# A streaming encoder layer: rotation partners of queries and keys moved 64 partitions apart, query norms taken up in the scores' scale

## The chip, the cores and the metric

One NeuronCore of one Trainium2 chip runs the whole layer in one launch. The metric is the device time of that launch in microseconds (us), the median of several runs. A profiled execution is one more run, with the hardware profiler's records; its span goes from the first to the last instruction.

## The reference, cut to what matters

The kernel computes one layer for 1024 prompt tokens and 32 tokens of a running stream, 1056 in all: two token mixers (windowed attention with sinks, a gated linear recurrence), their merge, and a SwiGLU feed-forward part. Everything is float32. The part that the change touches is what happens to queries and keys between the input projection and the attention scores:

```python
q = partial_rope(rms_norm(q.reshape(B, T, N_HEADS, HEAD_DIM), q_norm), positions)
k = partial_rope(rms_norm(k.reshape(B, T, N_KV_HEADS, HEAD_DIM), k_norm), positions)
# rms_norm: x * rsqrt(mean(x*x) + 1e-6) * gain, over the 64 features of a head
# partial_rope: of the 64 features, the first 16 are rotated, feature d (0..7) with its partner d+8
x1, x2 = xr[..., : ROT_DIM // 2], xr[..., ROT_DIM // 2:]
rot = jnp.concatenate([x1 * cos - x2 * sin, x2 * cos + x1 * sin], axis=-1)
# attention: each chunk of 64 tokens sees its own chunk and the one before
s = jnp.einsum('bnqkgd,bnskd->bnkgqs', q, k).astype(jnp.float32) * ATTN_SCALE
m = jnp.maximum(jnp.max(s, axis=-1, keepdims=True), sink)
p = jnp.exp(s - m)
den = jnp.sum(p, axis=-1, keepdims=True) + jnp.exp(sink - m)
```

There are 16 query heads and 4 key and value heads of 64 features, so four groups of four query heads share one key head.

## The kernel before, in words

Activations lie by features: 128 features on the partitions, 1056 tokens along the free dimension, cut into three blocks of 352 tokens (`BW`). A float32 product is made of three TensorE products of a split form (high times high, high times low, low times high); GpSimd makes the high and low parts of each weight unit (128 x 1024 numbers) in `split` (L494), in two halves of 512, one rounding copy (L501) and one subtraction (L503) each. Two units are held, so a unit can be split once the unit two before it has been used up. The first 52 units (`EARLY`) are split so; a block of 352 tokens of one unit is `dense_block` (L589): 24 products of 128x128 weights with 352 columns.

The stages, in order of time: loads and the first norm; four rounds of the recurrence's front; the values (nine jobs on tokens as rows); six blocks of keys (two units of 128 features, each with two heads, times three token blocks); six blocks of queries for group 0; then, for each of the four groups, four units of merge gates (288 products, `group`, L754) with the attention of the group woven in between them, and after each of the first three groups the six query blocks of the next one. From about 694 us on come the large output and feed-forward products. The order of all work is written out by hand in the program of each engine, with semaphores between them.

Around the change, for one block k of keys or queries:

- ScalarE, `qk_copy` (L1034): the squares of the block into `qsq` (L1040), the block times the norm's gain into `qsb` (L1041); both have two buffers, and the copy of block k waits until the rotation products and the cosine product of block k-2 have been done.
- TensorE, `qk_aux` (L691), after the next dense block: two plain float32 products of 352 columns, with `blkones` (ones on each head's 64 x 64 block: sums of squares, already spread over the head's partitions) into `aux0`, and with `perm` (a signed permutation: each feature's rotation partner) into `aux1`. Each is recorded as two matmuls with a weight load of its own.
- ScalarE, `qk_root` (L1043): the square root of the mean into `qstd`.
- VectorE, `rope` (L1458): partner times sine from `aux1` (L1462), `qsb` times cosine (L1463), their sum (L1466), the reciprocal of `qstd` (L1468), and the product with it, into `kst` for keys (L1476) or into `qt` for queries (L1482).

Keys go through DRAM (`store_k`, L1048) and come back per group into `kg` (`load_group`, L1076), which holds two copies of the group's key head, one on the upper and one on the lower 64 partitions, with zeros elsewhere (set once, L1486 and L1487), so that one product gives the scores of two heads. An attention step (`attention_step` in the programs of TensorE L715, ScalarE L1096 and VectorE L1494) handles one chunk u of 64 tokens: scores, row maxima (L1508), the negated maximum with the sink (L1515), `exp` with the scale 1/8 (L1111), the row sums and their reciprocal, the scaled probabilities (L1519), two steps later their transposes (L750), three steps later the product with the values. Steps begin with the 72nd of the group's 288 products and then come every 11 products. `small1` and `small2` hold constants, among them `blkones`, `perm`, the gains and the sinks.

## Time and profile before

| what | us |
|---|---|
| median of 3 runs | 1694.2 |
| the 3 runs | 1694.5, 1689.61, 1694.2 |
| profiled execution, its own time | 1689.04 |
| its span, first to last instruction | 1687.0 |

The granted TensorE clock over the span is 0.992 of full speed. The page of the profile gives the busy time of each engine; matmuls are pipelined, so that a matmul's recorded duration is longer than the distance from its start to the start of the next one. The distance between starts is what TensorE spends.

### The profile page before, as it was taken

How to read it: one execution, taken by the hardware profiler on the slowest of the kernel's cores; microseconds unless marked ns; L12 is line 12 of the kernel's file. 1: busy time of each engine (PE TensorE's matmuls, PEld its weight loads, DVE VectorE, ACT ScalarE, POOL GpSimd, SP SyncE). 2: the span in 40 equal slices, each digit the busy share in tenths (PEclk: the TensorE clock that was granted, in tenths of full speed). 3: DMA queues.
4: the chain of work that ended last, by engine and by line, in shares of the span. 5: the costliest groups of instructions: out<-in, count | busy, mean ns of one | idle time of the engine just before them, and what ended most of it. 6: DMA issues, size and time to landing. Idle time of an engine off the chain costs nothing. (4 is left out here: it accounts for less than half of the span.)

```text
span 1687.0 us, 29106 instructions
## 1 busy us (share of the span) xinstructions
PE 1630.2 (97%) x11242; PEld 1538.5 (91%) x11242; DVE 1056.0 (63%) x1648; ACT 621.0 (37%) x1310; POOL 958.3 (57%) x685
## 2 busy tenths in 40 slices
PE   7899989999999999999898999999999999999999
PEld 4799989988889898898897989999999999998998
DVE  6687674964747565667889778333333334869685
ACT  5444542243343424424234334333333334333242
POOL 5665652222223121377785717877777777786876
PEclk9999999999999999999999999999999999999999
DMA  5011122233123131254441612222242222373634
GB/s 191 26 63 63 57 68 83 67 90 103 55 85 75 68 102 57 99 217 166 153 154 56 200 52 87 91 77 78 81 167 95 77 77 77 141 265 115 254 141 148
DMA packets 72764, 182.12 MB, mean 108 GB/s; under 512 B 14704, under 2 KB 26416, under 8 KB 72000
## 3 DMA queue, kind: packets, MB, share of 16 engines
q1 hardware_dynamic: 51376, 159.13, 26.8%
q10 hardware_dynamic: 21264, 21.27, 4.4%
q8 instruction: 85, 1.39, 0.3%
q14 instruction: 39, 0.32, 0.1%
HBM read 131.36 MB, written 49.28 MB: 107 GB/s over the span
## 5 line engine op out<-in xcount | busy, mean ns | idle before, releaser
L577 PE MATMUL bank<-xh,wsh 128*128 128x264 f32 x2170 | 623.4, 287 | 21.7 <-POOL wsl L553 8.1
L577 PE MATMUL bank<-xh,wsl 128*128 128x264 f32 x2170 | 619.8, 286 | 0.0
L577 PE MATMUL bank<-xl,wsh 128*128 128x264 f32 x2170 | 619.2, 285 | 0.0
L577 PEld LDWEIGHTS bank<-xh,wsh 128*128 128x128 f32 x2170 | 411.5, 190 | 25.3 <-issue 16.1
L577 PEld LDWEIGHTS bank<-xl,wsh 128*128 128x128 f32 x2170 | 411.5, 190 | 0.2
L577 PEld LDWEIGHTS bank<-xh,wsl 128*128 128x128 f32 x2170 | 411.7, 190 | 0.0
L577 PE MATMUL bank<-acth,wh 128*128 128x352 f32 x960 | 320.6, 334 | 4.6 <-POOL actl L509 3.7
L577 PE MATMUL bank<-acth,wl 128*128 128x352 f32 x960 | 311.7, 325 | 0.0
L577 PE MATMUL bank<-actl,wh 128*128 128x352 f32 x960 | 310.2, 323 | 0.0
L501 POOL TENSOR_SCALAR wh<-wraw 128x512 fp32r<-128x512 f32 x100 | 83.7, 837 | 393.6 <-PE bank L577 373.5
L553 POOL TENSOR_TENSOR wsl<-praw,wsh 128x512 fp32r<-128x512 f32 (+1 forms) x157 | 242.5, 1545 | 81.2 <-ACT wsh L1166 81.1
L553 POOL TENSOR_TENSOR wsl<-wsum,wsh 128x512 fp32r<-128x512 f32 (+1 forms) x120 | 186.2, 1552 | 84.8 <-ACT wsh L1166 84.7
L1166 ACT ACTIVATE wsh<-praw 128x512 fp32r<-128x512 f32 (+1 forms) x157 | 97.0, 621 | 260.7 <-PE bank L577 234.9
L577 PEld LDWEIGHTS bank<-acth,wh 128*128 128x128 f32 x960 | 180.3, 188 | 9.5 <-POOL actl L509 4.5
L577 PEld LDWEIGHTS bank<-actl,wh 128*128 128x128 f32 x960 | 180.9, 188 | 3.2
L577 PEld LDWEIGHTS bank<-acth,wl 128*128 128x128 f32 x960 | 180.3, 188 | 0.4
L503 POOL TENSOR_TENSOR wl<-wraw,wh 128x512 fp32r<-128x512 f32 x100 | 148.3, 1483 | 14.6 <-POOL wh L501 0.2
L1741 DVE TENSOR_TENSOR ev<-bank,ev 128x264 f32<-128x264 f32 x126 | 53.8, 431 | 158.9 <-PE bank L577 158.9
L1166 ACT ACTIVATE wsh<-wsum 128x512 fp32r<-128x512 f32 (+1 forms) x120 | 74.2, 619 | 197.6 <-POOL wsum L549 117.0
L1548 DVE TENSOR_TENSOR xl<-acc,xh 128x2112 fp32r<-128x2112 f32 (+1 forms) x47 | 129.7, 2759 | 23.9 <-ACT xh L1183 23.9
L1645 DVE SCALAR_TENSOR_TENSOR ev<-bank,ev 128x264 f32<-128x264 f32 x90 | 38.7, 430 | 136.0 <-PE bank L577 135.3
L549 POOL TENSOR_TENSOR wsum<-praw,wsum 128x512 f32<-128x512 f32 (+1 forms) x45 | 73.2, 1627 | 79.9 <-PE bank L577 79.9
(173 smaller groups left out, 2393.2 us busy)
## 6 DMA issues: line engine op xcount, KB each, us to landing
praw<-in_weights SPq DMA_DIRECT2D x34, 1024.0 KB, 4.8
wraw<-in_weights SPq DMA_DIRECT2D x52, 512.0 KB, 3.3
h_scratch<-ev SPq DMA_DIRECT2D x44, 264.0 KB, 2.0
acc<-h_scratch SPq DMA_DIRECT2D x4, 2112.0 KB, 12.5
ev<-x_scratch SPq DMA_DIRECT2D x6, 1056.0 KB, 4.9
spare<-x_scratch SPq DMA_DIRECT2D x6, 1056.0 KB, 5.0
praw<-in_weights SPq DMA_DIRECT2D x8, 768.0 KB, 4.6
ta_scratch<-tg ACTq DMA_DIRECT2D x24, 176.0 KB, 1.8
```

Of the source, the lines that this page charges most:

```text
L501: nc.gpsimd.tensor_scalar(wh[:, u, c], wraw[:, u, c], 1.0, 0.0, ALU.mult, ALU.add).then_inc(split_done, 1)
L503: nc.gpsimd.tensor_tensor(wl[:, u, c], wraw[:, u, c], wh[:, u, c].bitcast(f32), ALU.subtract)\
L549: nc.gpsimd.tensor_tensor(dst, a, b, op).then_inc(wsum_done, 1)
L553: nc.gpsimd.tensor_tensor(w_slot(wsl, p, r), w_part(p, r), w_slot(wsh, p, r).bitcast(f32), ALU.subtract)\
L577: return nc.tensor.matmul(*args, **kw)
L1166: f(w_slot(wsh, p, r), w_part(p, r), ACT.Copy).then_inc(whi_done, 1)
L1548: V.tensor_tensor(xl[k][:, 0:n, :], x_part(t, k), xh[k][:, 0:n, :].bitcast(f32), ALU.subtract)\
L1645: stt(u2(par, n), bank[BANKS[2][n]][:, 0:QB], scale, u2(par, n), ALU.mult, ALU.add).then_inc(u2_done, 1)
L1741: V.tensor_tensor(dst, bank[BANKS[r][n]][:, 0:QB], (u4(par, n), None, u2(par, n), u2(par, n))[r - 3], ALU.add).then_inc(done, 1)
```

## The change

The features of two heads, which lay as head 0 on partitions 0 to 63 and head 1 on 64 to 127, are laid out anew: of each run of 16 features the first eight go to the lower 64 partitions and the second eight to the upper 64, so that feature d and its partner d+8 lie exactly 64 partitions apart. Head 0 then has partitions 0 to 31 and 64 to 95, head 1 the rest. GpSimd makes this order as it splits the weight units of keys and queries (ten of the 52; the loop over units is written out from the 14th pair of units on). VectorE reads the partner from the other half of the partitions, so the `perm` product is gone. Keys keep their norm as before, with the ones matrix `heads` in the new pattern, now made on the chip. Queries are no longer divided by their norm: ScalarE squares them into a part of `ot` that is free at the time, 17 small products per group sum them (tokens as rows, two columns), and the inverse root comes into the scores' scale and into the negated maximum. Loads and stores that meet the features' order (rotation tables, gains, cached keys, key outputs) are cut up accordingly.

```diff
-KVG_DMAS = 16 * 7
+KVG_DMAS = 16 * 9
+PAIR_ROWS = ROT // 2
+TURNED = (13, 14, 17, 20, 23)
+    def turned(rows):
+        return rows.rearrange("(a s b) t -> s a b t", s=2, b=PAIR_ROWS)
-        small2 = tensor(early, "small2", [P, C_END - C_BLK])
+        small2 = tensor(early, "small2", [P, C_END - C_VEC])
+        heads = tensor(early, "heads", [P, P])
+        gains = tensor(early, "gains", [P, 2])
+            qroot = tensor(s, "qroot", [P, AU, 2])
+            qinv = tensor(s, "qinv", [P, 2, AU, 2])
+        def qsquares(g):
+            return ot[:, g % 2, :, :].rearrange("p i t -> p (i t)")
+        def by_unit(a, n, i):
+            return a[:, 2 * n * BW:2 * (n + 1) * BW].rearrange("p (b i t) -> p b i t", i=2, t=HT)[:, :, i, :]
 GpSimd
+            def turn(half):
+                return half.rearrange("p (c a s b) -> p s c a b", c=4, s=2, b=PAIR_ROWS)
+            def straight(half):
+                return half.rearrange("p (c s a b) -> p s c a b", c=4, s=2, b=PAIR_ROWS)
+                    if turned:
+                        raw, high, low = turn(raw), straight(high), straight(low)
 TensorE
-            def qk_aux(base, k, b, after):
-                wait(pe, free[b], after)
-                wait(pe, std_done, base + k)
-                mm(aux0[:, 0:BW], blkones, qsq[:, k % 2, :], start=True, stop=True).then_inc(ss_done, 1)
-                wait(pe, rot_used, base + k)
-                mm(aux1[:, 0:BW], perm, qsb[:, k % 2, :], start=True, stop=True).then_inc(rot_done, 1)
+            def k_sums(k, b, after):
+                wait(pe, free[b], after)
+                wait(pe, std_done, k)
+                mm(aux0[:, 0:BW], heads[:, :], qsq[:, k % 2, :], start=True, stop=True).then_inc(ss_done, 1)
+            def q_sums(g, job):
+                wait(pe, free[job.bank], job.after)
+                wait(pe, std_done, 6)
+                wait(pe, qroot_done, 2 * g)
+                wait(pe, ot_done, AU * g)
+                for u in range(AU):
+                    q, _, q0 = unit_shape(u)
+                    i = mm(aux0[0:2 * q, 2 * u:2 * u + 2], qsquares(g)[:, 2 * q0:2 * (q0 + q)], heads[:, 0:HD:HD // 2],
+                           start=True, stop=True)
+                i.then_inc(qss_done, 1)
-                    if done[0] == 9:
-                        qk_aux(*late)
+                    if done[0] == 18:
+                        q_sums(g, late)
 ScalarE
-            act.dma_start(kt_dram[:, SEQ:SEQ + KV_CACHED], kc_in[:, WINDOW - KV_CACHED:WINDOW]).then_inc(kv_stored, 16)
+            for i in range(2):
+                for h in range(2):
+                    rows = slice(i * P + h * HD, i * P + (h + 1) * HD)
+                    for j in range(2):
+                        r0 = i * P + j * HD + h * HD // 2
+                        act.dma_start(kt_dram[r0:r0 + HD // 2, SEQ:SEQ + KV_CACHED].rearrange("(a b) t -> a b t", b=PAIR_ROWS),
+                                      turned(kc_in[rows, WINDOW - KV_CACHED:WINDOW])[j]).then_inc(kv_stored, 16)
-            act.dma_start(cs[:, :, :], cs_in).then_inc(cs_loaded, 16)
+            for j in range(2):
+                act.dma_start(cs[j * HD:(j + 1) * HD, :, :].rearrange("p k t -> p (k t)"),
+                              turned(cs_in.rearrange("p k t -> p (k t)"))[j]).then_inc(cs_loaded, 16)
+                wait(act, cos_done, base + k - 1)
+                f(qsb[:, k % 2, :], ps, ACT.Identity, scale=gain).then_inc(copied, 1)
+                if base == 0:
+                    wait(act, ss_done, k - 1)
+                    f(qsq[:, k % 2, :], ps, ACT.Square).then_inc(free[job.bank], 1)
+                else:
+                    g = base // 6 - 1
+                    wait(act, ot_stored[g % 2], 16 * (g // 2))
+                    f(by_unit(qsquares(g), k % NB, k // NB), ps.rearrange("p (b t) -> p b t", t=HT), ACT.Square)\
+                        .then_inc(free[job.bank], 1)
+            def q_root(g):
+                    wait(act, qss_done, g + 1)
+                    wait(act, qinv_done, 4 * g)
+                    f(qroot[rows, units, :], aux0[rows, 2 * units.start:2 * units.stop].rearrange("p (u h) -> p u h", h=2),
+                      ACT.Sqrt, scale=1.0, bias=HD * EPS).then_inc(qroot_done, 1)
-                        f(pr[0:2 * q, r, h, 0:k], sbank[i % 2][0:2 * q, h * P:h * P + k], ACT.Exp, scale=HD ** -0.5,
+                        f(pr[0:2 * q, r, h, 0:k], sbank[i % 2][0:2 * q, h * P:h * P + k], ACT.Exp,
+                          scale=qinv[0:2 * q, 0, i, h:h + 1],
-                qk_root(6 * g + 6, 5)
+                q_root(g)
 VectorE
-                V.tensor_tensor(rt2[:, :], aux1[:, 0:BW], cs[:, 1, x], ALU.mult).then_inc(rot_used, 1)
+                stt(rt2[0:HD, :], qsb[HD:P, k % 2, :], -1.0, cs[HD:P, 1, x], ALU.mult, ALU.mult).then_inc(sin_done, 1)
+                stt(rt2[HD:P, :], qsb[0:HD, k % 2, :], 1.0, cs[0:HD, 1, x], ALU.mult, ALU.mult).then_inc(sin_done, 1)
             def rope_q(base, k):
-                rope(base, k)
+                halves(base, k)
+                V.tensor_tensor(by_unit(qt, k % NB, k // NB), rt1[:, :].rearrange("p (b t) -> p b t", t=HT),
+                                rt2[:, :].rearrange("p (b t) -> p b t", t=HT), ALU.add).then_inc(rope_done, 1)
+            def q_inverse(g):
+                    V.reciprocal(qinv[rows, 0, units, :], qroot[rows, units, :]).then_inc(qinv_done, 1)
+                    V.tensor_scalar(qinv[rows, 1, units, :], qinv[rows, 0, units, :], -1.0, None, ALU.mult).then_inc(qinv_done, 1)
-            V.memset(kg[HD:P, 0, :], 0.0).then_inc(kz_done, 1)
-            V.memset(kg[0:HD, 1, :], 0.0).then_inc(kz_done, 1)
+            for j in range(4):
+                V.memset(kg[j * HD // 2:(j + 1) * HD // 2, 1 - j % 2, :], 0.0).then_inc(kz_done, 1)
-                    stt(sm[rows, r, 1, :], sm[rows, r, 0, :], -HD ** -0.5, snk[rows, 0, :], ALU.mult, ALU.min)\
+                    for h in range(2):
+                        stt(sm[rows, r, 1, h:h + 1], sm[rows, r, 0, h:h + 1], qinv[rows, 1, i, h:h + 1], snk[rows, 0, h:h + 1],
+                            ALU.mult, ALU.min).then_inc(nm0_done, 1)
 SyncE
+            for j in range(2):
+                sp.dma_start(gains[j * HD:(j + 1) * HD, :], turned(small_in[:, C_GAIN:C_SINK])[j]).then_inc(gains_loaded, 16)
...
```

## Rows read from the trace of the kernel before

**Rows 1.** The page's first part: busy time, share of the span, instructions.

```profile
PE 1630.2 (97%) x11242; PEld 1538.5 (91%) x11242; DVE 1056.0 (63%) x1648; ACT 621.0 (37%) x1310; POOL 958.3 (57%) x685
```

**Rows 2.** Busy time by stretch: its ends and length, engines, granted clock, DMA.

```profile
404.00:438.00 34.00, 34.00 (x193) 31.45 (x193) 22.12 (x24) 10.94 (x21) 12.60 (x12) 1.00 0.44 107
...
694.00:1687.00 993.00, 965.37 (x7236) 937.35 (x7234) 606.56 (x767) 338.52 (x553) 706.45 (x457) 0.99 0.37 130
```

**Rows 3.** Timeline of TensorE around one pair of small products: start, us, engine, line.

```profile
326.78 0.32 PE L577 MATMUL bank<-actl,wh 128*128 128x352 f32 x1
...
330.33 0.32 PE L577 MATMUL bank<-acth,wl 128*128 128x352 f32 x1
330.49 0.75 PE L577 MATMUL bank<-qsq,small 128*128 128x352 f32 x2
...
331.83 0.32 PE L577 MATMUL bank<-actl,wh 128*128 128x352 f32 x1
...
336.86 0.32 PE L577 MATMUL bank<-actl,wh 128*128 128x352 f32 x1
```

**Rows 4.** Timeline of TensorE: pairs in the queries of group 1.

```profile
412.14 0.76 PE L577 MATMUL bank<-qsq,small 128*128 128x352 f32 x2
...
432.27 0.75 PE L577 MATMUL bank<-qsq,small 128*128 128x352 f32 x2
```

**Rows 5.** Weight loads: one tile's (ns min/median/max), then a stretch of the timeline.

```profile
L577 PEld LDWEIGHTS bank<-qsq,small x60: 187/188/190, 284.2 to 627.7; 128*128 128x128 f32 x60
...
378.41 0.19 PEld L577 LDWEIGHTS bank<-acth,wl 128*128 128x128 f32 x1
378.52 0.19 PEld L577 LDWEIGHTS bank<-acth,wh 128*128 128x128 f32 x1
```

**Rows 6.** Timeline of VectorE, and of ScalarE's square, in one block of keys.

```profile
304.33 0.53 DVE L1462 TENSOR_TENSOR rt<-bank,cs 128x352 f32<-128x352 f32 x1
304.77 0.52 DVE L1463 TENSOR_TENSOR rt<-qsb,cs 128x352 f32<-128x352 f32 x1
...
306.17 0.46 ACT L1040 ACTIVATE qsq<-bank 128x352 f32<-128x352 f32 x1 [4.08 <-PE bank L577]
...
308.90 0.53 DVE L1462 TENSOR_TENSOR rt<-bank,cs 128x352 f32<-128x352 f32 x1
```

**Rows 7.** Timeline of VectorE and GpSimd at the start of the keys.

```profile
288.50 0.99 DVE L1487 MEMSET kg<- 64x1120 f32 x1 [0.29 <-issue]
...
290.43 1.37 POOL L503 TENSOR_TENSOR wl<-wraw,wh 128x512 fp32r<-128x512 f32 x1
290.75 1.43 DVE L1466 TENSOR_TENSOR rt<-rt 128x352 f32<-128x352 f32 x1
```

**Rows 8.** Timeline of ScalarE at the start, and one later store.

```profile
0.74 0.65 ACTq L890 DMA_DIRECT2D kt_scratch<-in_cache_k  x1
...
2.73 1.28 ACT L896 ACT_TABLE_LOAD   x1 [2.73 <-issue]
...
6.59 2.44 ACT L923 ACTIVATE wg<-wraw,vt 128x128 f32<-128x128 f32 x8 [2.11 <-DMA wraw<-in_weights]
...
305.59 0.45 ACTq L1058 DMA_DIRECT2D out_ks<-kst  x1
```

**Rows 9.** Timeline of GpSimd: a split half, before the keys and in group 1.

```profile
277.05 1.29 POOL L503 TENSOR_TENSOR wl<-wraw,wh 128x512 fp32r<-128x512 f32 x1
...
446.44 0.62 POOL L501 TENSOR_SCALAR wh<-wraw 128x512 fp32r<-128x512 f32 x1 [9.02 <-PE bank L577]
```

**Rows 10.** Timeline of VectorE and TensorE in a running attention step.

```profile
378.52 0.42 DVE L1519 TENSOR_TENSOR pr<-pr,sm 128x256 f32<-128x256 f32 x1
...
381.18 0.44 PE L750 MATMUL bank<-small,pr 128*128 128x128 f32 x2
```

**Rows 11.** Busy time by stretch (as in Rows 2), around a long stall of TensorE.

```profile
764.00:766.00 2.00, 0.00 (x0) 0.00 (x0) 2.00 (x2) 1.00 (x2) 2.00 (x2) 0.85 0.06 23
...
768.00:770.00 2.00, 2.00 (x11) 2.00 (x11) 0.89 (x1) 0.00 (x0) 2.00 (x2) 0.50 0.91 372
```

More of the change, by code:

```diff
@@ L516, in _ @@
             x_low(2)
-            with pool.Fori(2, EARLY_N // 2) as i:
+            with pool.Fori(2, TURNED[0]) as i:
                 for u in range(2):
                     split(i, u, False)
+            for i in range(TURNED[0], EARLY_N // 2):
+                for u in range(2):
+                    split(i, u, False, i in TURNED)
             def w_sum(p, i):
@@ L587, in products, with dense_block @@
                 return mm(out, lhs[1], rhs[0][cols], start=False, stop=last)
-            def dense_block(slot, n, rh, rl, each=None, ahead=0, before=None):
+            def dense_block(slot, n, rh, rl, each=None):
                 job = plan.take(last=n == NB - 1)
@@ L594, in dense_block @@
                     if n == 0 and k % 4 == 0:
-                        weights(ahead, k // 4)
-                    if before:
-                        before(n, k)
+                        weights(0, k // 4)
                     w = slice(k * P, (k + 1) * P)
@@ L702, in qk @@
                         job = dense_block(i, n, acth, actl)
-                        if attended is not None and i == 0 and n == 1:
-                            wait(pe, pt_done, attended)
-                            wait(pe, ot_done, attended)
                         if late:
-                            qk_aux(*late)
-                        late = (base, NB * i + n, job.bank, job.after)
-                return late
-            late = qk(0)
-            late = qk(6, late)
+                            k_sums(*late)
+                        late = (NB * i + n, job.bank, job.after) if keys else None
+                return late or job
+            def q_sums(g, job):
[8 more added lines that the diff above has]
+                i.then_inc(qss_done, 1)
+            pe.wait_ge(heads_done, 5)
+            late = qk(keys=True)
+            late = qk(late)
             def attention_step(g, i):
@@ L1488, in _ @@
+            V.memset(heads[:, :], 0.0).then_inc(heads_done, 1)
+            dve.wait_ge(heads_done, 1)
+            for j in range(4):
+                rows = slice(j * HD // 2, (j + 1) * HD // 2)
+                V.memset(heads[rows, :].rearrange("p (s h n) -> p h s n", s=2, h=2)[:, j % 2], 1.0).then_inc(heads_done, 1)
+            dve.wait_ge(cs_loaded, 32)
+            for j in range(4):
+                V.memset(kg[j * HD // 2:(j + 1) * HD // 2, 1 - j % 2, :], 0.0).then_inc(kz_done, 1)
             for k in range(6):
```

115 lines of the change are left out of this document (56 added, 59 removed).

## The prediction

> **What bounds the kernel now.** I read the page's busy shares first: TensorE works 97% of the span, no other engine above 63% [rows 1], and the granted clock is 1.00 where the change lies and 0.99 in the long stage behind it [rows 2]. So time is won where TensorE spends less, and lost where it waits. Next the timeline of TensorE in a query phase: 22 dense products start between 326.78 and 330.33, 0.161 us apart, so a block of 24 takes 3.87. Then the pair of small products comes: from 330.33 to 331.83 it is 1.50 us for what would be two steps (0.32), so a pair costs 1.18 us, 0.59 a product, in float32 with two passes each [rows 3]. The queries of group 1 bear it out: pairs 0 and 4 stand 20.13 us apart, 5.03 a block, and 5.03 - 3.87 = 1.16 [rows 4]. Third, VectorE beside it: one key block takes it 4.57 us, from the first row to the last [rows 6]. It is just below TensorE's 5.03, so today it keeps up, and it is the engine to watch when TensorE's blocks get shorter. The stage after 694 us starts from TensorE's end of the groups, and TensorE is busy 965 of its 993 us [rows 2]: I let it move as it is.
>
> **Queries, groups 1 to 3.** Each group had six pairs: 6 x 1.17 = 7.0 us go. What comes is 17 products with a stationary operand of 128 squares' columns and two moving columns, two passes each as for every plain float32 product (x2 in [rows 3]), so 34 weight loads with next to nothing between them. The trace has no such series. From below: nothing under the 0.06 us that would be half of the load distance below, 2.0 us a group. From above: a load takes 0.188 us from start to end [rows 5], 6.4 us a group if none overlaps. Nearest is a place where the queue was empty and two full loads follow each other, 378.41 and 378.52: 0.11 us apart [rows 5]; the second began as soon as the first was in place. I take 0.11 plus 0.01 for the short product, 0.12 x 34 = 4.1 us. So a group gains 7.0 - 4.1 = 2.9 us, three groups 8.7.
> VectorE falls from five operations to four short ones per query block: each 0.44 from the next or 0.53 long [rows 6], and not over 0.2 of semaphores between them, about 2.3 us against 3.87, so no query block waits for it. ScalarE's root moves behind the sums: it comes some 7 us into the group, while the first attention step is at product 72, 11.6 us plus the 4.1 in; the two reciprocals and negations are tiny. Cost nothing; cover 8 us.
>
> **Keys and queries of group 0.** A key block keeps one product: TensorE's pace could be 3.87 + 0.59 = 4.46. VectorE now needs 4.57 + 0.44 for the second half of the sine product = 5.01 [rows 6]. So here VectorE becomes the bound: TensorE's sums of block k wait for ScalarE's copy of k, and that waits for the cosine product of k-2. VectorE starts later too: the second memset of `kg` started at 288.50 and lasted 0.99 [rows 7]; there are now four of them, so with 0.4 for the second table load they end about 288.5 + 0.4 + 3 x 0.99 + 0.3 = 292.2. The sums of the sixth key block then need the cosine product of the fourth: 292.2 + 3 x 5.01 + 1.4 (0.44 + 0.44 + 0.52) = 308.6; ScalarE's two operations of 0.46 [rows 6] 0.9, the sums 0.6: 310.1; GpSimd's contention (below) 0.6: 310.7. Five query blocks more are 19.35: group 0 starts at 330.1. Before it started one product ahead of 336.86, at 336.7 [rows 3]. That is 6.6 us gained, and up to product 72 there is 4.1 now against 1.17: 3.7 net. If TensorE kept its own pace of 4.46 through five key blocks, it would be up to 2.8 us better; if each key block cost VectorE 0.5 more, 1.5 to 2.5 worse.
>
> **Start.** ScalarE issues ten loads at the head of its program in place of three, each of its DMA issues from DRAM to DRAM 0.65 us [rows 8]; a store with several strides is 0.45 [rows 8]. Eight by 0.45 to 0.65 replace one: 3.0 to 4.6 us more ahead of the table load at 2.73. That work used to end 2.11 us before the first weights landed at 6.59 [rows 8], so 0.9 to 2.5 us are late, and ScalarE's scaled weights are what the first matmul waits for. I take 1.6 lost. The smaller constant load may give back 0.3.
>
> **GpSimd's new order.** A half takes 0.62 for the copy and 1.29 for the subtraction [rows 9], in runs of 512; the ten turned units read runs of eight. The trace has no such access on this engine. From below no gain (same count of elements); from above I let it take three times as long, 5.7 us a half. Before the query units GpSimd had been idle 9.02 us [rows 9], so even 3 x as long costs little there. The first key unit is not covered, as TensorE waits for its halves: 1.9 us more for each doubling of a half, but VectorE's bound in the keys (start at 292.2) hides about 2.5 us of that. I take 0 (runs of 32 bytes, same engine work), bound 4.
>
> **Attention steps.** One more tiny operation on VectorE (0.1 us) ahead of `exp`. A chunk's probabilities are ready at 378.52 + 0.42 = 378.94 and transposed at 381.18 [rows 10]: 2.2 us of slack. Nothing.
> What works against this cover: in the keys' rows a sum on VectorE lasted 1.43 in place of 0.53 while GpSimd's subtraction ran from 290.43 to 291.80 [rows 6, 7]. The change replaces an operation with one operand in PSUM by two with both in SBUF, so it meets this more often: at most 0.9 us per meeting, two units split in the keys, 0.6 to 2 us; the 0.6 is in the sum above. The Trainium skill (SBUF — State Buffer, section "SBUF: two separate sides") says that the port pair shared by VectorE and GpSimd is an exclusive lock, taken by a VectorE operation with two SBUF inputs; the trace agrees with the 1.43 us. By that rule alone every one of the eight GpSimd operations in the keys would be added to VectorE, and the keys would end 2 us later still.
>
> **Sum.** 8.7 + 3.7 - 1.6 + 0.3 = 11.1 us less. On the profiled execution, 1689.0 - 11.1 = 1677.9. The median shown is 5.2 us above that execution and the fastest run 0.6 above it, so the runs alone scatter by 0.3%, about what a measurement of this kernel can tell from no change; I put the median after at 1694.2 - 11.1 = 1683.
>
> **Rivals.**
> A. The clock falls. In the 4.1 us of the sums TensorE multiplies next to nothing. After a stall in which it stood still (busy 0.00 from 764 to 766), the granted clock went from 1.00 to 0.50, the lower level of 1.2 GHz, and stayed there while it was fully busy from 768 to 770 [rows 11]. Such a fall costs half of some 3.4 us, 1.7 us. Four groups: 6.8 us, so the gain is 4.3 and the time 1690. For it: the products' columns are too few to count. Against it: weights are loaded all the time, and the dense products stand right before and behind. The Trainium skill (TensorE: Matmul & The Clock Gate, "What's actually happening") says that the throttled state is the default and activity releases it; it agrees with the rows, and doesn't settle whether loading counts.
> B. Loads that don't overlap (ends slower). Each small pass waits for its own load to end and the load for the pass before: 0.188 plus some 0.06 of the product, 0.25 us, 136 of them 34 us in place of 16.3. That takes 17.7 us back: slower by 6.6, 1701. It decides from 11.1 + 16.3 = 27.4 us over 136, 0.20 us a pass. For it: the 0.188 of the load [rows 5]. Against it: the 0.11 there.
> C. The loads are cheaper, 0.06 to 0.08 us a pass: 6 to 8 us better, 1676.
> D. The change does less than it says: VectorE's keys and the start cost 5 us more (three times as long turned splits, 0.65 a DMA issue, port waits): 1688.
>
> **How the numbers follow.** Forecast 0.40, A 0.28, B 0.08, C 0.12, D 0.12. The likeliest is 1683. C sets the low end, 1673; A and D with a median that may itself fall 3 us either way set the high end, 1693. Faster by over 0.3% (below 1689): the forecast and C nearly whole, half of D and 0.4 of A, 0.40 + 0.12 + 0.06 + 0.12 = 0.70. Slower: B and a rest of D and A, 0.10. Same 0.20.
>
> **What would show it.** TensorE's count falls by 54 products and rises by 68. The weight loads with `ot` as source stand 0.11 us apart (C: 0.06; B: 0.2 or more). In the keys VectorE has no idle time from about 292 us on, and TensorE waits for ScalarE's square there, some 3 us in all. Query blocks start 3.87 us apart. The first matmul starts 1 to 2 us later than 9.13. Granted clock 1.00 between 320 and 690 (A: below it in four places right behind the sums). Group 0's attention starts about 345 us. The forecast is wrong if the loads cost over 0.16 us each, or if TensorE waits in the query phases for any engine.

## The result, and the profile after

The changed kernel takes 1699.01 us (median of 6 runs, 1698.15 to 1700.86) against 1692.9 before (6 runs, 1689.61 to 1694.5). The ratio is 1.0046 with a 95% interval of 1.0034 to 1.0057: slower by 0.46%. The forecast was 1683 with a range of 1673 to 1693, so it missed, and on the wrong side. The profiled execution has a span of 1696.7 us against 1687.0, and a mean granted clock of 0.984 against 0.992.

The first part of the page, as in [rows 1]: TensorE is busy 5.6 us less in a span that is 9.7 us longer. It waits more.

```profile
PE 1624.6 (96%) x11270; PEld 1544.6 (91%) x11270; DVE 1031.9 (61%) x1721; ACT 626.4 (37%) x1294; POOL 959.2 (57%) x685
```

Three marks on TensorE's timeline divide the difference: the first score product of group 0, the first product of the stage behind the groups, and the end of the span. Before they stand at 349.69, 694.85 and 1687.0, after at 363.13, 707.02 and 1696.7. So up to the first score 13.4 us are lost, in the four groups 1.3 are won (345.16 to 343.89), and behind them 2.5 come back (992.15 to 989.68). By its sum the prediction had 2.4 us won by the first mark (3.7 - 1.6 + 0.3; its "about 345 us" for the first score would be 4.7 and does not fit that sum), and 8.7 between the first two.

Two things limit this account. The profiled execution of the kernel before is its fastest (1689.04 by its own time, median 1692.9), that of the changed kernel lies at its median, so the marks divide 9.7 us where the medians differ by 6.1. And the code behind the groups is the same in all fourteen kernels of this document, while that stage lasts 989.6 to 993.5 us in their traces: the 2.5 us are within that scatter.

**Start.** Timeline of ScalarE (ACT, its DMA queue ACTq) and TensorE (columns: start, us, engine, line), beside [rows 8]:

```profile
0.74 6.96 ACTq L930 DMA_DIRECT2D kt_scratch<-in_cache_k  x8
7.74 0.63 ACTq L932 DMA_DIRECT2D out_ks<-in_cache_k  x1
...
9.26 1.28 ACT L937 ACT_TABLE_LOAD   x1 [9.26 <-issue]
...
10.92 2.43 ACT L964 ACTIVATE wg<-wraw,vt 128x128 f32<-128x128 f32 x8
...
13.44 0.93 PE L606 MATMUL bank<-acc,wg 128*128 128x352 f32 x1 [13.44 <-ACT wg L964]
```

Eight issues take 0.87 us each. The table load starts 6.5 us later than before, the scaled weights 4.3 later, and the first product at 13.44 in place of 9.13.

**Keys.** Timeline of all engines in the keys of group 0; compare the starts with [rows 6, 7]:

```profile
285.17 1.41 ACTq L1073 DMA_DIRECT2D cs<-in_rope  x2
...
297.50 0.99 DVE L1562 MEMSET kg<- 32x1120 f32 x1 [25.79 <-DMA cs<-in_rope]
298.78 0.99 DVE L1562 MEMSET kg<- 32x1120 f32 x1 [0.28 <-issue]
...
302.36 0.52 DVE L1523 SCALAR_TENSOR_TENSOR rt<-qsb,cs 64x352 f32<-64x352 f32 x1
...
305.49 1.51 PE L606 MATMUL bank<-qsq,heads 128*128 128x352 f32 x2 [7.67 <-ACT qstd L1097]
...
307.62 0.52 DVE L1523 SCALAR_TENSOR_TENSOR rt<-qsb,cs 64x352 f32<-64x352 f32 x1
...
319.65 0.66 ACTq L1118 DMA_DIRECT2D out_kp<-kst  x1
...
322.37 0.56 ACT L1084 ACTIVATE qsb<-bank,gains 128x352 f32<-128x352 f32 x1 [6.51 <-DVE rt L1525]
...
323.77 1.51 PE L606 MATMUL bank<-qsq,heads 128*128 128x352 f32 x2 [3.11 <-ACT qstd L1097]
```

The rope tables are issued 3.2 us later than before (285.17 against 281.99) and land 12.3 us after that in place of 5.2. The four zeroings stand 1.28 apart, as the two did before (the forecast had 0.99), and the first product of the rotation starts at 302.36 in place of 289.42. TensorE stands still for 7.67 us and then for 3.11: ScalarE's chain is held by VectorE, and before the second stall by six stores besides. Both sums last 1.51 us where 0.75 is usual [rows 3]; the clock has fallen to its lower level. The 18 products ahead of group 0's sums put the start of group 0 at 346.2.

While the tables come in, half of the DMA engines' time is busy, against nearly all of it before (stretches as in [rows 2], the last two numbers are the DMA engines' busy share and GB/s; first the changed kernel, then the one before):

```profile
291.00:296.00 5.00, 5.00 (x31) 4.79 (x31) 0.00 (x0) 0.00 (x0) 2.34 (x3) 1.00 0.50 145
```

```profile
283.00:287.00 4.00, 4.00 (x24) 3.58 (x23) 0.00 (x0) 1.57 (x4) 0.00 (x0) 1.00 0.93 339
```

**Sums of the queries.** Timeline of TensorE and its weight loads at group 0's sums:

```profile
348.95 3.91 PEld L606 LDWEIGHTS bank<-heads,ot 128*128 128x128 f32 x34
...
349.11 3.83 PE L606 MATMUL bank<-heads,ot 128*128 128x2 f32 x34
...
353.51 0.50 PE L606 MATMUL bank<-acth,wh 128*128 128x352 f32 x1
...
353.80 0.50 PE L606 MATMUL bank<-actl,wh 128*128 128x352 f32 x1
```

The 17 products are 34 passes, each with its own weight load; they take 3.83 us, 0.113 each, close to the 0.12 forecast. Dense products then start 0.29 us apart and not 0.16. The stretches behind the four bunches (columns as in [rows 2]; the granted clock is the third number from the end):

```profile
350.00:352.00 2.00, 2.00 (x20) 2.00 (x19) 1.86 (x3) 0.00 (x0) 1.41 (x1) 1.00 0.81 192
...
354.00:356.00 2.00, 2.00 (x9) 2.00 (x8) 1.49 (x8) 0.99 (x2) 0.00 (x0) 0.50 0.57 198
...
448.00:452.00 4.00, 4.00 (x19) 3.97 (x19) 0.90 (x7) 1.99 (x4) 0.00 (x0) 0.62 0.40 131
...
544.00:548.00 4.00, 4.00 (x17) 3.97 (x17) 0.61 (x4) 1.99 (x4) 0.00 (x0) 0.57 0.26 103
...
640.00:644.00 4.00, 4.00 (x17) 3.98 (x17) 0.61 (x4) 1.99 (x4) 0.00 (x0) 0.57 0.96 353
```

TensorE is busy all the time, and the clock still goes from 1.00 to 0.50, that is from 2.4 to 1.2 GHz, behind every bunch.

**First attention step.** Timeline at group 1's first scores (458.85):

```profile
459.88 1.28 POOL L530 TENSOR_TENSOR wl<-wraw,wh 128x512 fp32r<-128x512 f32 x1
...
460.05 1.14 DVE L1600 TENSOR_TENSOR sm<-sm,snk 128x2 f32<-128x2 f32 x1
...
462.23 0.92 DVE L1577 TENSOR_TENSOR sm<-sm 128x2 f32<-128x2 f32 x1 [1.04 <-ACT sm L1175]
...
463.99 0.15 DVE L1600 TENSOR_TENSOR sm<-sm,snk 128x2 f32<-128x2 f32 x1
464.12 0.70 PE L606 MATMUL bank<-kg,qt 128*128 128x256 f32 x2 [0.94 <-DVE pr L1595]
```

Two operations on two columns last 1.14 and 0.92 us beside GpSimd's split; the same one takes 0.15 without it.

### The profile page after: what moved, and what is told of

It reads as the page before. It is cut to its first block and busy times, and to the rows that moved or that the text cites. A ratio compares the mean times of both kernels' runs of the same rounds, so it can differ in the third digit from the quotient of the medians.

```text
span 1696.7 us, 29002 instructions
## 1 busy us (share of the span) xinstructions
PE 1624.6 (96%) x11270; PEld 1544.6 (91%) x11270; DVE 1031.9 (61%) x1721; ACT 626.4 (37%) x1294; POOL 959.2 (57%) x685
## 5 line engine op out<-in xcount | busy, mean ns | idle before, releaser
L606 PE MATMUL bank<-acth,wl 128*128 128x352 f32 x960 | 315.3, 328 | 0.0
L606 PE MATMUL bank<-actl,wh 128*128 128x352 f32 x960 | 314.2, 327 | 0.0
L582 POOL TENSOR_TENSOR wsl<-praw,wsh 128x512 fp32r<-128x512 f32 (+1 forms) x157 | 254.3, 1619 | 84.8 <-ACT wsh L1226 84.7
L606 PEld LDWEIGHTS bank<-acth,wh 128*128 128x128 f32 x960 | 183.9, 192 | 7.4 <-POOL actl L535 4.4
L606 PEld LDWEIGHTS bank<-actl,wh 128*128 128x128 f32 x960 | 184.3, 192 | 0.9 <-issue 0.5
L606 PEld LDWEIGHTS bank<-acth,wl 128*128 128x128 f32 x960 | 183.7, 191 | 0.4
## 6 DMA issues: line engine op xcount, KB each, us to landing
acc<-h_scratch SPq DMA_DIRECT2D x4, 2112.0 KB, 12.3
```

What stands on the lines that cost most here:

```text
L582: nc.gpsimd.tensor_tensor(w_slot(wsl, p, r), w_part(p, r), w_slot(wsh, p, r).bitcast(f32), ALU.subtract)\
L606: return nc.tensor.matmul(*args, **kw)
```

## The experiments

E1 to E12 are in the order of the sections. "Marks" are the first score of group 0 and the first product behind the groups. The kernel before ran beside each lot and had medians of 1690.85 (E1 to E4), 1689.69 (E5 to E8), 1690.41 (E9, E10), 1691.75 (E11) and 1690.24 (E12). The changed kernel itself ran only in the first comparison, where the kernel before had 1692.9. So a difference of medians against its 1699.01, as given below, can hold up to 2 us between the lots. By the ratios the gains of E1 to E4 are 3.2, 4.1, 5.6 and 7.4 us in place of 3.7, 4.1, 6.6 and 7.9.

E2, E4 to E9, E11 and E12 take the tables in the rotated order from the host, all but E2 the gains and cached keys as well, and give the keys back in that order: the reordering is then outside the measured launch. Only the changed kernel, E1, E3 and E10 make the order on the chip. E5 to E9, E11 and E12 have woven sums unless the text says otherwise. In E7 and E9 to E12 the first attention step, and with it the first mark, stands eight dense products (1.3 us) earlier.

| kernel | median us (runs) | ratio to before, 95% | marks |
|---|---|---|---|
| E1 cache copies later | 1695.3 (7) | 1.0027, 1.0016 to 1.0039 | 359.87, 703.69 |
| E2 one table load | 1694.92 (10) | 1.0022, 1.0011 to 1.0034 | 357.75, 701.43 |
| E3 sums woven | 1692.43 (10) | 1.0013, 1.0003 to 1.0022 | 359.56, 699.24 |
| E4 order on the host | 1691.12 (10) | 1.0002, 0.9992 to 1.0012 | 353.06, 696.96 |
| E5 = E4 + E3 | 1685.55 (10) | 0.9974, 0.9960 to 0.9989 | 351.87, 691.53 |
| E6 zeros earlier | 1682.36 (7) | 0.9959, 0.9938 to 0.9980 | 349.57, 689.22 |
| E7 first step earlier | 1682.83 (10) | 0.9951, 0.9933 to 0.9969 | 353.44, 692.43 |
| E8 one sine product | 1676.36 (4) | 0.9917, 0.9894 to 0.9941 | 345.32, 685.04 |
| E9 three buffers | 1689.97 (12) | 0.9998, 0.9985 to 1.0011 | 356.49, 695.45 |
| E10 order on the chip | 1685.01 (10) | 0.9966, 0.9954 to 0.9978 | 349.44, 688.51 |
| E11 ScalarE exchanges | 1673.8 (5) | 0.9897, 0.9880 to 0.9914 | 344.65, 683.29 |
| E12 = E11, sums in a bunch | 1682.0 (4) | 0.9951, 0.9934 to 0.9967 | 345.28, 686.55 |

**E1.** The eight copies of cached keys go behind the first scaled weights.

```
-            for i in range(2): for h ...: for j in range(2):   # kt_dram <- turned(kc_in), 8 DMAs
             act.dma_start(ks_out[:, 0:WINDOW - DEC], ...)
...
+            (the same eight, behind the loop that scales wg)
```

> The changed kernel, with its eight loads of cached keys issued by ScalarE behind the recurrence stage instead of at the head of its program; all else as changed. Theory (the start costs what the trace of the changed kernel shows): the first matmul goes back from 13.44 to about 9.1 us and the whole run is 4.3 us faster than the changed kernel, 1694.7. Rival (the start is bound by the loads of x, and ScalarE's delay is partly hidden by them): the first matmul is early again, but under 2 us of it reach the end. Nothing changes in the keys or in the clock of the groups.

The first product starts at 9.2 and the median falls by 3.7 us. What the start lost reached the end of the span nearly whole.

**E2.** The tables are put into the rotated order on the host and loaded at once.

```
-            for j in range(2):
-                act.dma_start(cs[j * HD:(j + 1) * HD, ...], turned(cs_in...)[j]).then_inc(cs_loaded, 16)
+            act.dma_start(cs[:, :, :], cs_in).then_inc(cs_loaded, 16)
```

> The changed kernel, with the rotation tables laid out in the new feature order in DRAM beforehand, so that one load of 128 partitions brings them as in the kernel before; all else as changed. Theory (the keys are late because the two loads of 64 partitions landed 12 us after their issue, against 5.0 for the one before): VectorE's zeroing of kg starts at about 290.5 instead of 297.5, TensorE's 7.67 us stall goes, with it one of the falls of the clock: 7 to 9 us faster than the changed kernel, about 1691. Rival (VectorE's pace of 5.25 us a key block is the bound all the same, from its four memsets on): the load lands early but TensorE stalls later by as much, and under 3 us are won.

The load is issued at 283.95 and landed at 291.05, 7.1 us against 12.3. 4.1 us are won, less than expected: TensorE's waits for the root go from 10.8 to 5.8 us and not away, since the four zeroings and VectorE's pace stay. A wait of 1.10 us for the last queries' squares comes in right ahead of the first bunch of sums, and behind it the clock is low for 7 us.

**E3.** The 17 sums stand one behind every second dense product, in place of all in a row.

```
-                    if done[0] == 18:
-                        q_sums(g, late)
+                    if done[0] >= 18 and done[0] % 2 == 0 and done[0] < 18 + 2 * AU:
+                        q_sum(g, late, (done[0] - 18) // 2)
```

> The changed kernel, with the 17 small products of squares of a group put one behind every second dense product, from the 18th on, instead of all behind the 18th; all else as changed. Theory (rival A of the prediction: the 3.8 us of loads with nothing to multiply let the clock fall, 3.4 us at half speed in each of four groups): the granted clock stays 1.00 in the groups and the run is 4 x 1.7 = 6.8 us faster, 1692. Rival 1 (the clock falls for another reason, the stalls in the keys): clock and time as in the changed kernel. Rival 2 (each change between dense and small products costs some 0.1 us more on TensorE): 68 x 0.1 us eat the gain and the time stays 1699 though the clock is 1.00.

6.6 us less, and the granted clock is 1.00 from 350 to 710 us. From group to group the first scores are 94.3 us apart, against 95.7 in a bunch and 96.42 before. The same work costs 1.4 us less a group: rival A. The fall itself costs a little more than that, as E12 will show.

**E4.** Tables, gains and cached keys in rotated order on the host, and the results put back there: one cache copy, four stores per end block, one load of the tables.

```
-            (8 copies of cached keys, 2 table loads, 2 loads of gains, 6 stores of an end block)
+            act.dma_start(kt_dram[:, SEQ:SEQ + KV_CACHED], kc_in[:, WINDOW - KV_CACHED:WINDOW])...
+            act.dma_start(kp_out[rows, :], kst[:, slot, a - WINDOW:a])...
```

> The changed kernel, with every array that meets the feature order (rotation tables, gains, cached keys, key outputs) in the new order in DRAM, so that loads and stores are whole again: one load of cached keys, one of tables, four stores for a last key block instead of six, no loads of gains of their own. All else as changed. Theory (start and keys together): first matmul at about 9.1 us, 4.3 won; tables early, 7 to 9 won; the second stall in the keys (ScalarE issues six stores of 0.6 us ahead of a copy) shorter by 1.5 to 3: 13 to 16 us faster than the changed kernel, 1683 to 1686, with the clock still falling behind the sums in each group. Rival (the parts hide one another): less than 10 us.

It won 7.9 us, of 13 to 16. The first rotation product still waits for four zeroings (284.45 to 289.31), and TensorE waits four times for the root, 5.0 us in all. So VectorE was the bound of the keys there too, as E2 had said. A further part of what is missing stands ahead of the first bunch of sums: with the keys shorter, TensorE waits there for the last queries' squares, and the clock is low for 10 us behind it. Timeline of TensorE, then busy time by stretch:

```profile
335.81 5.82 PE L606 MATMUL bank<-heads,ot 128*128 128x2 f32 x34 [1.92 <-ACT ot L1082]
```

```profile
338.00:346.00 8.00, 8.00 (x33) 7.97 (x34) 3.38 (x11) 1.99 (x4) 0.00 (x0) 0.50 0.76 143
```

**E5.** Both edits together.

> The changed kernel with both earlier edits at once: every table and cache in the rotated row order on the host (no 64-partition loads, no eight cache copies, four stores per key block), and the 17 sums of a group each two dense products apart. Theory (the two losses are separate and add): host order alone came to 1691.1 us, and weaving alone took 6.6 us off the changed kernel, so 1684.5 us, TensorE's clock 1.00 from 350 to 710 us. The steps from group to group, first score to first score, were 95.7 us with the sums in a bunch and 94.3 woven: 4 x 1.4 = 5.7 of the 6.6. Rival (the clock that weaving saved was lost only because of the stalls in the keys in front of group 0, so they overlap): only three falls are saved, 1686.8 us or more.

1685.55: the two losses nearly add (1691.12 less 6.6 is 1684.5). By the ratios weaving is worth 4.7 us here and 5.6 in E3.

**E6.** E5, and the zeroings go ahead of the wait for the tables, into idle time.

```
-            dve.wait_ge(cs_loaded, 16)
+            dve.wait_ge(unit_done, 6 * GROUPS)
             (four memsets of kg)
+            dve.wait_ge(cs_loaded, 16)
```

> As the kernel before it, and the four zeroings of the group's key tile are moved from behind the table's landing to a place 20 us ahead, where VectorE has idle time. Theory (VectorE bounds the keys): the four are 1.28 us apart with the first product of the rotation 4.9 us behind the first zeroing, and TensorE then waited 5.0 us in four places for ScalarE's root, which waits for VectorE. With VectorE 4.9 us earlier nearly all of that goes, and part of the clock loss behind it (0.94 in 262 to 350 us): 4.0 to 6.0 us less than the kernel before it, about 1680. Rival (the first key block's copy, not VectorE's start, is the limit): VectorE then waits for ScalarE's copy, gain 2 us or less, 1682.5 or more.

3.2 us less than E5, a little under the forecast 4 to 6, and the executions lie wide apart, from 1678.5 to 1687.7. In the profiled one (1681.9) TensorE still waits 2.1 us once for the root. So VectorE is still just the bound there.

**E7.** E6, and each group's first attention step moves from dense product 72 to 64.

```
-    return START_MM + SLOT_MM * i
+    return START_MM + SLOT_MM * i - 8 * (i == 0)
```

> As the kernel before it, and the first attention step of each group stands behind dense product 64 in place of 72; the other steps stay. In all kernels so far GpSimd splits a unit of weights right when product 72 is done, and in the changed kernel two tiny VectorE operations of the first step lasted 1.14 and 0.92 us beside it in place of 0.15, after which TensorE waited 0.9 to 1.0 us for the probabilities (before: 0.3), and 0.4 us for the attention output. Theory (the longer chain of the change meets GpSimd's split): those waits fall from 5.4 us to 1 or 2 in the four groups, 3 to 4 us less, 1676.5. Rival (the chain of exp with a per-partition scale and one more VectorE operation is too long by itself at every step): waits stay, within 0.5 us of the kernel before it.

The step from group to group is 93.8 us, 0.5 less than in E6, so 1.9 for four groups; the wait for probabilities goes from 3.8 to 1.8 us, that for the output stays (1.7). That is half of the forecast 3 to 4. The median does not show it, as the executions lie wide apart again (1675.4 to 1687.3). In the profiled one (1684.7) TensorE waits 2.12 us for the root at 309.48, which costs no clock, and 1.92 us for the last queries' square, right ahead of the woven sums. Timeline of TensorE, then busy time by stretch:

```profile
334.18 0.38 PE L606 MATMUL bank<-heads,ot 128*128 128x2 f32 x2 [1.92 <-ACT ot L1083]
```

```profile
336.00:352.00 16.00, 16.00 (x63) 15.60 (x63) 3.74 (x12) 2.24 (x5) 0.00 (x0) 0.50 0.41 80
352.00:354.00 2.00, 2.00 (x13) 2.00 (x12) 0.08 (x1) 0.11 (x1) 0.00 (x0) 0.78 0.26 90
354.00:358.00 4.00, 4.00 (x26) 3.95 (x26) 1.53 (x9) 1.33 (x6) 2.56 (x4) 1.00 0.12 45
```

The clock stays at 0.50 for 17 us and comes back only when the sums have ended (the last starts at 349.32): over 8 us for a wait of 1.9. In E6, where the 2.12 us stood in the keys ahead of 312.67, it averaged 0.67 and 0.90 in the two stretches of 4 us behind. Weaving does not help behind such a wait: with the same 1.92 us ahead of a bunch (E4) the clock was low for 10 us, ahead of woven sums for 17.

**E8.** E6, and one sine product over 128 partitions in the keys. It takes each feature itself in place of its partner: the rotation of the keys is left out, and the kernel only prices the work.

```
-                stt(rt2[0:HD, :], qsb[HD:P, ...], -1.0, cs[HD:P, 1, x], ...)
-                stt(rt2[HD:P, :], qsb[0:HD, ...], 1.0, cs[0:HD, 1, x], ...)
+                stt(rt2[:, :], qsb[:, k % 2, :], 1.0, cs[:, 1, x], ...)
```

> As the second kernel of this call (zeroings moved), with one sine product over 128 partitions without exchange in place of the two of 64 partitions, in the keys only: the rotation of keys is left out, the rest is computed. It prices what the second half product costs where VectorE bounds. Theory (VectorE at 5.25 us a key block against TensorE's 4.46): the lead of 4.9 us just covers five blocks at 0.8 each, so 0.55 a block less gives 0 to 1 us. Rival (VectorE bounds the keys from the first block on in that kernel too): 5 x 0.55 = 2.7 us less.

6.0 us less than E6, more than either account gave. In the profiled execution the stall is gone, and the clock's fall with it: 1.00 in 280 to 420 us. All four executions lie close together (1675.45 to 1678.17). VectorE's key blocks are 5.2 us apart in place of 6.05 in E6, so 0.85 less and not 0.55: fewer of its operations meet GpSimd's splits as well.

**E9.** E7, and a third buffer for the keys' copy and root.

```
-                wait(act, cos_done, base + k - 1)
+                wait(act, cos_done, base + k - (1 if base else 2))
-                wait(act, rope_done, k - 1)
+                wait(act, rope_done, k - 2)
```

> As the kernel with the first attention step moved, and a third buffer each for the scaled copy and the root of the keys (in the attention's probability tile, idle there), so that ScalarE's copy and root of a block wait for VectorE's third block back and not its second. The executions of the two kernels before it fall into two groups, about 1676 to 1679 and 1681 to 1687 us, and in the profiled ones (both of the longer kind) TensorE once waits 2.1 us in the keys for the root and the granted clock falls behind it (0.76 in 320 to 350, 0.91 in 300 to 320). Theory (VectorE still bounds the keys by a little, and a stall of 2 us costs as much again or more in clock): with 5 us more slack the stall and the fall go in every execution, median 1676 to 1677 us, granted clock 1.00 from 300 to 350. Rival (the bound is VectorE's total work in the keys, or the stores, not the buffers): the stall moves to a later place and both kinds of executions stay, median 1680 or more.

My theory fell, and the rival stood: 7 us slower than E7. Timeline of VectorE, GpSimd and TensorE in E9:

```profile
315.49 0.88 DVE L1537 TENSOR_TENSOR kst<-rt,qstd 128x352 f32<-128x352 f32 x1
...
316.09 1.44 POOL L540 TENSOR_TENSOR wl<-wraw,wh 128x512 fp32r<-128x512 f32 x1
...
316.48 1.43 DVE L1522 SCALAR_TENSOR_TENSOR rt<-pr,cs 64x352 f32<-64x352 f32 x1
...
318.79 1.51 DVE L1524 TENSOR_TENSOR rt<-pr,cs 128x352 f32<-128x352 f32 x1
...
329.45 0.40 PE L616 MATMUL bank<-acth,wh 128*128 128x352 f32 x1 [2.76 <-POOL wl L540]
...
336.05 0.59 PE L616 MATMUL bank<-heads,ot 128*128 128x2 f32 x2 [3.48 <-ACT ot L1093]
```

TensorE runs through the keys without a wait, and so GpSimd splits its units while VectorE works: operations of 0.53 last 1.4 to 1.5, and six key blocks take 38.3 us, 6.4 each. The debt falls due at GpSimd's split and at the last queries' squares, both of which are late, and behind the second the clock is at 0.50 from 336 to 355 us, much as in E7. So it is VectorE's total work, what GpSimd adds to it included, that bounds this stretch, and not a buffer.

**E10.** As E9, with the order made on the chip as in the change (but the copies of the cached keys behind the first scaled weights, as in E1).

> As the kernel before it in this call but with the changed kernel's own handling of the rotated order on the chip: the rope table by two loads of 64 partitions, the cached keys by eight DMAs (behind the first scaled weights and not ahead of them), six stores per end key block. Theory (the table's landing 12 us behind its issue in place of 5, and two more issues of a store on ScalarE, are what the order on the chip costs once start, zeroings, sums and buffers are mended): VectorE starts the keys 8 to 10 us later, five key blocks can't make it up, TensorE waits 5 to 8 us in the keys and the clock falls behind: 1683 to 1687 us. Rival (three buffers hide the late table as well): within 2 us of the kernel before it.

1685.01, 5 us faster than E9. It was meant to price the order on the chip, but the two kernels stall in different places, so the difference does not give that price. Its waits are 2.06 us for the root of the third block (L1109), as ScalarE's copy for it had waited 8.27 us for VectorE, and 3.07 behind six stores; both come in the keys, and the clock is back at 1.00 from 320 on. It is the fastest kernel here that makes the order on the chip: 0.34% faster than the kernel before.

**E11.** E7 (two buffers), and in the keys ScalarE writes the exchanged copy, and VectorE multiplies once.

```
+                    f(exchanged(k)[0:HD, :], ps[HD:P, :], ACT.Identity, scale=gain[HD:P, :])
+                    f(exchanged(k)[HD:P, :], ps[0:HD, :], ACT.Identity, scale=gain[0:HD, :])
...
+                    stt(rt2[:, :], exchanged(k), signs[:, 0:1], cs[:, 1, x], ALU.mult, ALU.mult)
```

> The kernel with the first attention step moved (two buffers as there), and the exchange of the two halves of the partitions made in the keys by ScalarE: two scaled copies of 64 partitions from PSUM, with a column of signs for VectorE's then single sine product over 128 partitions. What three buffers showed: VectorE took 38.3 us for six key blocks, 6.4 a block and not 5.0, as seven or eight of its operations with two operands in SBUF lasted 1.3 to 1.5 us beside GpSimd's splits in place of 0.53, and the stall only moved to the last queries (3.5 us for the squares, 2.8 for GpSimd). Theory (VectorE's total work from the first key to the last query of group 0 is the bound): 0.55 us less in each of six blocks, 3.3 us, takes that bound below TensorE's pace as leaving the exchange out did (1676.4 us, all executions within 3), and the moved first step gives another 1.9: 1674 to 1676 us. ScalarE's two more operations of some 0.45 us a block fit into its idle time (4.7 us busy of 20). Rival (ScalarE is then late with the squares and the copies, two in a row before the square that frees the PSUM bank): TensorE waits for ScalarE in the keys, 1680 or more.

1673.8 us (1672.44 to 1675.92): 1.0% faster than the kernel before, and the best of all, with the order made on the host. Busy time by stretch; TensorE waits nowhere in the keys for ScalarE or VectorE, and the clock stays up:

```profile
300.00:320.00 20.00, 20.00 (x122) 19.36 (x121) 18.70 (x22) 6.90 (x15) 4.80 (x6) 1.00 0.25 79
320.00:350.00 30.00, 30.00 (x199) 29.69 (x197) 20.98 (x40) 7.31 (x19) 11.52 (x11) 1.00 0.36 94
```

**E12.** E11 with the sums of a group in one bunch again.

> The kernel with ScalarE's exchange, its sums put back in one bunch of 17 per group as the change has them. It asks the first question again where nothing else stalls ahead of the sums. Theory (the granted clock falls behind each bunch, and only for that): 1.4 us a group from group to group, 5.6 in all, median 1679.4, granted clock 1.00 from 280 to 345 and below 1.00 just behind each of four bunches. Rival (the clock falls only if a stall came shortly ahead): 1674 to 1676.

8.2 us slower, against 5.6 expected. The stretches behind the first and the fourth bunch:

```profile
337.00:342.00 5.00, 5.00 (x24) 5.00 (x24) 2.27 (x9) 1.71 (x2) 0.00 (x0) 0.68 0.49 127
...
620.00:626.00 6.00, 6.00 (x44) 5.97 (x44) 1.09 (x7) 2.00 (x4) 0.00 (x0) 1.00 0.75 261
```

No stall stood ahead of the first bunch, and the clock fell all the same, so the bunch alone does it. It fell behind three of the four: the first scores of groups 0 to 2 are 95.2 us apart, and those of groups 2 and 3, with the fourth bunch between them and no fall, 93.55, which is 0.2 less than woven (93.75). So a fall costs 1.6 us (95.2 less 93.55), and weaving, which avoids it, costs 0.2 for 17 products: together the 1.4 of E3. In the profiled executions the marks account for 3.3 us of the 6.0 between the spans; the other 2.7 lie behind the groups, in the stage that scatters by up to 3.9 us between traces. That three falls of 1.6 and a median 8.2 us slower belong together is not shown: where the rest comes from stays open, as does what spares one bunch.

## Why the prediction was wrong

**Start: mis-sized.** The step took 0.45 to 0.65 us a DMA issue and 1.6 lost. The issue costs 0.87 with this pattern of DRAM rows, and 4.3 were lost (E1: 3.7 in the median). Seven more issues at 0.87 are 6.1, less the 2.1 of slack it names: 4.0. The form of the term was right, and the upper end of its price for an issue too low.

**VectorE's start in the keys: mis-sized, the largest term.** "They end about 288.5 + 0.4 + 3 x 0.99 + 0.3 = 292.2" against 302.36: 10.2 us. One thing was left out, one priced far too low and one a little. The start's own loss moves the issue (3.2 left out). Two loads of 64 partitions land 7.1 us later after their issue than the one before, and I had priced the second by its issue alone, 0.4 (6.7 short). The zeroings stand 1.28 apart and not 0.99, which the second of [rows 7] had shown in its idle time; from the second of them to the first product that is 3.6 us and not 3.3 (0.3 short). 3.2 + 6.7 + 0.3 = 10.2. Against the kernel before, whose first product starts at 289.42, the same terms are 3.2 + 7.1 + 2.7 for two more zeroings: 13.0, the 12.9 seen. The Trainium skill (DMA: Bandwidth & Descriptors, section "Why a DMA increments its semaphore by 16 and not by 1") says that a transfer runs on the largest number of DMA engines up to 16 that divides the slowest dimension of both patterns; for this pattern of 8 by 8 rows that is 8. The trace agrees: the DMA engines' busy share is 0.50 from 291 to 296, and 0.93 from 283 to 287 in the kernel before. But no run changes the pattern with all else the same, so that the 12.3 us come from it is argued only.

**VectorE's pace in the keys: right that it is the bound, mis-sized.** 5.01 a block was forecast, and it is 5.25 alone (302.36 to 307.62), as small operations stand 0.55 apart and not 0.44. What GpSimd adds was put at 0.6 us in all. In the changed kernel the stalls kept the two engines mostly apart: from 307.0 to 335.2 the last operations of the six blocks are 5.6 apart. The less TensorE stalls, the more they meet: 6.05 apart in E6, 6.2 in E7, and 6.6 in E9, where it does not stall in the keys at all. The Trainium skill (SBUF — State Buffer, section "SBUF: two separate sides") calls the shared port pair an exclusive lock held for a whole instruction. E9's rows agree, and so does the 1.14 us of an operation on two columns: the price is by meeting, not by size. By its rule I had written that the keys would end 2 us later, and set it aside for 0.6; E9 shows that it was nearer.

**Sums: right.** 0.12 a pass forecast, 0.113 seen; 3.83 us a group against 4.1. Rivals B and C are out. The reading behind the 0.11 was not right: the second load of [rows 5] starts at 378.52, before the first one's recorded end at 378.60, and not when it was in place. The distance was the right row to take, all the same.

**Clock: rival A, at 0.28, was true.** All four bunches drop the clock, and so do 19 of the 20 bunches in the traces with bunched sums (the changed kernel, E1, E2, E4, E12). A fall costs 1.6 us (E12), and mending it by weaving gives back 1.4 a group (E3), where 1.7 was said. The 3.4 us behind that 1.7 stand in no row of the kernel before (around [rows 11] the clock stays low for 6 us); what the runs show in their place is the 1.6. I counted it as one rival beside the forecast, though nothing in the trace spoke for the clock holding: [rows 11] showed only that it falls, and there behind a stall.

**Attention steps: wrong.** "Nothing", with 2.2 us of slack from a running step [rows 10]. The first step of a group has no such slack. It meets GpSimd's split of the next unit, and TensorE waits 3.8 us for probabilities (1.1 before) and 1.6 for the output, 1.1 us more a group. E7 takes half of it back, so about half of it goes with the meeting; whether the rest is the longer chain (E7's rival) no run shows. So a group gains 7.0 - 3.8 for the products, less 1.4 and 1.1: 0.7, and the first scores are 95.7 apart in place of 96.42.

**GpSimd's turned order: right.** The copy and the subtraction of a turned half last 0.62 and 1.28 us (medians, 255 to 350 us), as in [rows 9].

**The sum.** Forecast 11.1 won; measured 9.7 lost in the profiled executions: 8.7 became 1.3, 2.4 for the start and the keys became a loss of 13.4, and 2.5 came back behind. Rivals A and D, which I had priced one at a time with 6.8 and 5 us, came together, and D was over three times as large. The step that failed is thus the term for VectorE's start in the keys, with the start ahead of it; the clock, put at nothing in the sum, and the attention steps come behind. The idea itself was sound: with the start, the zeroings, the sums, the first step and the exchange mended and the order made on the host, E11 is 18 us faster than the kernel before. With the order made on the chip the most that was measured is 5.4 us (E10); E11's exchange with that order was not run.

## What to carry to other kernels

Price a DMA with a new pattern by issue and by landing, with the late start of the engine that waits for its tile; and let losses ahead of a step move the step. When an edit shortens the bounding engine's work, sum up the next engine's whole work up to the point where all meet, at the length its operations have beside their neighbour, since stalls that go away let the two meet more often. Do not put work with few moving columns in a bunch on TensorE: spread between dense products it took 0.2 us more for 17 products and kept the clock, which was worth 1.6. In the two traces in which a wait of 1.9 or 3.5 us stood right ahead of the spread products it did not keep it, and 8 and 10 us more were lost. So look for such a wait first, and compare kernels over many executions: near the bound of an engine they lay up to 12 us apart.

## What the runs showed of the hardware

- 34 weight loads with products of two columns, 3.8 us, dropped the granted clock from 1.00 to 0.50 behind them with TensorE busy throughout; spread two dense products apart, they did not (E3, E5, E6, E8, E11). In 20 traced bunches it fell 19 times, and a fall cost 1.6 us. But where a wait of 1.9 us (E7) or 3.5 (E9) came right ahead of the spread ones, the clock stayed at 0.50 for 17 and 20 us and came back only after they had ended. Two stalls of 2.12 us in the keys cost no clock (E7) and under 2 us of it (E6).
- A VectorE operation of 128 x 2 elements with both operands in SBUF lasted 1.14 us beside GpSimd's subtraction of 1.28, and 0.15 without it.
- Eight DMA issues from DRAM to DRAM with rows in runs of eight took 0.87 us each on ScalarE's queue (0.74 in E2), the plain one 0.65.
- GpSimd's copy and subtraction of 128 x 512 elements lasted 0.62 and 1.28 us with the weights read in runs of eight, and 0.62 and 1.29 in runs of 512.
- `exp` over 128 columns with a scale per partition took 0.45 us in place of 0.36 (means of 120).
- While the two table loads of 64 partitions came in, the DMA engines were 0.50 busy, and the tables landed 12.3 us after their issue; with the one load of 128 partitions it was 0.93 and 5.2 us.
